# Rope pages and query blocks placed in memory that is free during the prompt attention, first page gathers issued there, and 16-row page gathers for some decode samples

## What is computed

```python
c_past = cache_kv_latent[i][page_table].reshape(db, past, KV_LORA)    # KV_LORA = 256
kr_past = cache_k_rope[i][page_table].reshape(db, past, ROPE_DIM)     # ROPE_DIM = 32
q_abs = jnp.einsum('bthn,chn->bthc', q_nope, w_uk)
s_past = jnp.einsum('bthc,bsc->bhts', q_abs, c_past) + jnp.einsum('bthr,bsr->bhts', q_rope, kr_past)
p = jax.nn.softmax(concatenate([s_past, s_new], -1) * scale, axis=-1)
o_lat = jnp.einsum('bhts,bsc->bthc', p[..., :past], c_past) + ...     # then times w_uv
```

## Time and profile before

| | |
|---|---|
| median of 3 runs | 1027.24 us (1026.8 to 1029.7) |
| profiled execution | 1029.6 us |
| its span | 1027.7 us |
| granted clock, mean of the span | 0.983 |
| busy share of the span: PE, DVE, ACT, POOL | 95%, 65%, 38%, 4% |
| prompt attention of the last head pair ends (DVE, attn_T) | 409.2 us |
| first score product of the sample loop | 415.74 us |
| last weighing of the sample loop | 533.9 us |
| indirect gathers: bytes, share of the 16 DMA engines over the span | 37.75 MB, 9.8% |

### The profile page before, as it was taken

The page is one execution under the profiler, slowest core; times in us unless marked ns, Lnnn a source line. Parts: engine busy times, 40 slices in busy tenths (PEclk is TensorE's granted clock), DMA queues, the critical chain, the costliest instruction groups (busy, mean ns, idle before and its releaser), DMA issues.

```text
span 1027.7 us, 22122 instructions
## 1 busy us (share of the span) xinstructions
PE 974.2 (95%) x9086; PEld 898.9 (87%) x9086; DVE 666.5 (65%) x1054; ACT 387.2 (38%) x857; POOL 39.1 (4%) x44
## 2 busy tenths in 40 slices
PE   4899999999999999599999999999999999999995
PEld 3899999988888897455569999999999999999995
DVE  7467556765555555888837658697774335767567
ACT  4234332324151514333323323556661124565331
POOL 0000000000000011333100000000000000000000
PEclk9899999999999999899999999999999999999998
DMA  9504444313233324999643934224323243341643
GB/s 256 169 24 106 122 122 108 89 23 102 50 96 85 105 102 158 383 344 354 243 161 118 281 85 125 82 82 115 90 82 93 81 114 83 94 111 56 190 119 124
DMA packets 174772, 136.88 MB, mean 133 GB/s; under 512 B 18707, under 2 KB 162936, under 8 KB 170328
## 3 DMA queue, kind: packets, MB, share of 16 engines
q1 hardware_dynamic: 166442, 93.47, 32.5%
q0 software_dynamic: 5760, 37.75, 9.8%
q10 hardware_dynamic: 2502, 4.68, 1.2%
HBM read 124.18 MB, written 11.80 MB: 132 GB/s over the span
## 4 chain that ended last, share of the span: by engine, by line
PE 78%; DVE 12%; issue 4%; ACT 3%; DMA 1%; ACTq 0%; DVEq 0%; another core or an unknown queue 0%; POOL 0%; POOLq 0%
PE PS L2014 34%; PE PS L2242 8%; PE PS L2694 8%; PE PS L2756 6%; PE PS L2025 3%; PE PS L2471 3%; DVE w_lo L1225 2%; PE PS L2589 2%; PE PS L2414 2%; ACT p_sample L972 2%; PE PS L2279 1%; PE PS L2268 1%; PE PS L2340 1%; DVE y_tok L1734 1%; PE PS L2256 1%
## 5 line engine op out<-in xcount | busy, mean ns | idle before, releaser
L2014 PE MATMUL PS<-x_hi,w_hi 128*128 128x262 f32 (+1 forms) x744 | 164.0, 292 | 2.7 <-DVE x_lo L1272 1.4
L1225 DVE TENSOR_TENSOR w_lo<-w_raw,w_hi 128x2048 fp32r<-128x2048 f32 (+3 forms) x65 | 125.9, 1937 | 59.7 <-ACT w_hi L703 48.2
L2014 PE MATMUL PS<-x_lo,w_hi 128*128 128x262 f32 (+1 forms) x744 | 160.0, 287 | 0.0
L2014 PE MATMUL PS<-x_hi,w_lo 128*128 128x262 f32 (+1 forms) x744 | 159.6, 286 | 0.0
L703 ACT ACTIVATE w_hi<-w_raw 128x2048 fp32r<-128x2048 f32 (+3 forms) x59 | 94.5, 1601 | 145.9 <-PE PS L2014 88.3
L2014 PEld LDWEIGHTS PS<-x_hi,w_hi 128*128 128x128 f32 x744 | 120.7, 190 | 6.0 <-issue 2.4
L2014 PEld LDWEIGHTS PS<-x_lo,w_hi 128*128 128x128 f32 x744 | 120.1, 190 | 0.0
L2014 PEld LDWEIGHTS PS<-x_hi,w_lo 128*128 128x128 f32 x744 | 120.0, 190 | 0.0
L2242 PE MATMUL PS<-x_hi,w_hi 128*128 128x262 f32 (+1 forms) x256 | 78.7, 307 | 0.0
L2242 PE MATMUL PS<-x_hi,w_lo 128*128 128x262 f32 (+1 forms) x256 | 73.3, 286 | 0.0
L2242 PE MATMUL PS<-x_lo,w_hi 128*128 128x262 f32 (+1 forms) x256 | 73.3, 286 | 0.0
(11 more groups left out here) (376 smaller groups left out, 2293.2 us busy)
## 6 DMA issues: line engine op xcount, KB each, us to landing
w_raw<-in_w_ffn_in_dram SPq DMA_DIRECT2D x44, 512.0 KB, 4.5
w_raw<-in_w_in_dram SPq DMA_DIRECT2D x37, 512.0 KB, 6.7
w_raw<-in_w_ffn_out_dram SPq DMA_DIRECT2D x28, 320.0 KB, 3.8
w_raw<-in_w_o_dram SPq DMA_DIRECT2D x12, 512.0 KB, 5.2
w_raw<-in_w_ffn_out_dram SPq DMA_DIRECT2D x16, 384.0 KB, 3.9
gate_scratch<-gate_out ACTq DMA_DIRECT2D x8, 524.0 KB, 2.9
gates<-gate_scratch SPq DMA_DIRECT2D x8, 524.0 KB, 9.0
x_T_scratch<-x_sum_T SPq DMA_DIRECT2D x1, 2144.0 KB, 7.5
```

The source lines that it names most:

```text
L1225: V.tensor_tensor(WL[:, at_, ks], RAW[:, at_, ks], WH[:, at_, ks].bitcast(F32), ALU.subtract).then_inc(s_wsplit, 1)
L2014: last = T.matmul(PS[:, bank, 0:n], w[:, par, kw + k, m * P:(m + 1) * P], x[:, k0 + k, half * n:(half + 1) * n], start=start and k == 0 an ...
```

## The change

Rope pages (PGR) and what lies behind them move up by 672 bytes, to 66208, behind q_heads. QBD leaves this row and goes behind the plan of the prompt attention (e3b), where nothing else lies; the gap that pages_c_first needed goes. A third table of row numbers, IDX4, is made for rows of 16 tokens, and `chunk_quad(b, c)` fetches four chunks with one indirect DMA, 16 KB for each partition, 2.1 MB in all. `chunks_in(b)` says which samples use it: 0, 3, 4, 6 and 7. Samples 1, 2 and 5 keep pairs.

On POOL, sample 0 is fetched by two gathers (the second after the 4th normalisation of the last head pair), rope page 0 follows at once, then pairs 0 and 4 of sample 1 after the 8th normalisation, pairs 2 and 6 after the 10th, and rope page 1 after the attention. From sample 2 the order is as before, with the waits for as many chunks as the gather brings; rope page b still stands behind the gather that brings chunks 2 and 3. On ACT the waits for the two gate stores move from the head of `spread_query` behind `stage_query(0)`. On DVE the memset of the new-token columns moves ahead of chunks 1 to 3 and has a count of its own, so that PE may start the scores before the gate stores have landed; PE waits for the other memset (`rows_set` 2) before the first weighing.

```diff
--- before.py
+++ after.py
@@ -115,6 +115,7 @@
             m[32 * g + HEADS + h, 86 + h] = 1.0
             if g < 3:
                 m[32 * g + h, 66 + h] = 1.0
+    m[:, 74:76] = 2 * (i % 4)[:, None] + np.arange(NCH // 4)[None, :]
     m[:, 82:86] = 4 * (i % 4)[:, None] + np.arange(NCH // 2)[None, :]
     c["small"] = m
     return c
@@ -207,6 +208,7 @@
         PTI = fixed("page_table_rows", [P, DEC], I32)
         IDX = fixed("page_rows", [P, DEC, NCH + 1], I32)
         IDX2 = fixed("page_pair_rows", [P, DEC, NCH // 2], I32)
+        IDX4 = fixed("page_quad_rows", [P, DEC, NCH // 4], I32)
         CN8 = fixed("latent_new_T", [P, 2, DEC])
         KR8 = fixed("rope_new_T", [P, DEC])
         arena = top[0]
@@ -257,13 +259,14 @@
         (EX, PTS), e3 = plan(e2, ("probs", [P, 2, 528]), ("probs_T", [P, 2, NT, P]))
 
         (PGC,), _ = plan(0, ("pages_c", [P, 2, NPAGES, KVL]))
-        (_, CTX, QAB, UV), e3b = plan(e3, ("gap5", [P, 392]), ("c_tok0", [T0, KVL]), ("q_abs", [P, 2, DEC, HEADS]), ("w_uv", [P, 2, 512]))
+        (CTX, QAB, UV), e3b = plan(e3, ("c_tok0", [T0, KVL]), ("q_abs", [P, 2, DEC, HEADS]), ("w_uv", [P, 2, 512]))
         assert PGC.shape[2] * KVL * 4 == 32768
-        (PGR, PB, SSM, OL, SPART, OPART, QBD, RTT), e4 = plan(
-            65536, ("pages_r", [P, 2, NPAGES, ROPE]), ("p_sample", [P, 2, 36, HEADS]),
+        (PGR, PB, SSM, OL, SPART, OPART, RTT), e4 = plan(
+            66208, ("pages_r", [P, 2, NPAGES, ROPE]), ("p_sample", [P, 2, 36, HEADS]),
             ("sm", [P, 2, 48]), ("o_lat", [P, 2, HEADS, DEC]),
-            ("score_parts", [P, 2, P]), ("out_parts", [P, 2 * KVL]), ("q_blocks", [P, 2, 9, 32]),
+            ("score_parts", [P, 2, P]), ("out_parts", [P, 2 * KVL]),
             ("rope_T", [P, 4, NCH, 32]))
+        QBD = at("q_blocks", e3b, [P, 2, 9, 32])
         (QRP,), _ = plan(102752, ("q_spread", [P, DEC, 9, HEADS]))
 
         slot_bytes = 8 * SLOT_W * 4
@@ -273,7 +276,7 @@
         assert 8 * KVL * 4 == slot_bytes
         CT = nc.alloc_sbuf_tensor_at("pages_T", [P, 4, 8, NCH, 32], F32, offset=base)
         assert NCH * 1024 * 4 <= 2 * KT * COLS * 4
-        assert e4 + 8 * KVL * 4 <= e3 + 392 * 4
+        assert e4 + 8 * KVL * 4 <= e3
 
         def page(b, c):
 
@@ -361,14 +364,19 @@
         s_pg = [[sem(f"pages_landed{j}_{c}") for c in range(2, NCH)] for j in range(2)]
         s_pf = [[sem(f"first_pages_landed{j}_{c}") for c in range(2)] for j in range(3)]
 
+        def chunks_in(b):
+
+            return 4 if b % 3 < 2 and b != 1 else 2
+
         def page_sem(b, c):
 
-            c -= c % 2
+            c -= c % chunks_in(b)
             return s_pf[b % 3][c] if c < 2 else s_pg[b % 2][c - 2]
 
         def page_count(b, c):
 
-            return b // 3 + 1 if c < 2 else b // 2 + 1
+            c -= c % chunks_in(b)
+            return b // 3 + 1 if c < 2 else len([d for d in range(b % 2, b + 1, 2) if c % chunks_in(d) == 0])
 
         S = sems
 
@@ -646,6 +654,7 @@
             turned = Count(S["ln_turned"])
             
             pair_rows = ins["cache_kv_latent"][0].rearrange("n (q r) c -> (n q) (r c)", q=16)
+            quad_rows = ins["cache_kv_latent"][0].rearrange("n (q r) c -> (n q) (r c)", q=8)
             rope_rows = ins["cache_k_rope"][0].rearrange("n (q r) c -> (n q) (r c)", q=4)
 
             def chunk_pair(b, c):
@@ -653,6 +662,13 @@
                 nc.gpsimd.indirect_dma_start(
                     out=page_pair(b, c).rearrange("p r c -> p (r c)"), out_offset=None,
                     in_=pair_rows, in_offset=bass.IndirectOffsetOnAxis(ap=IDX2[:, b, c // 2:c // 2 + 1], axis=0)
+                ).then_inc(page_sem(b, c), 16)
+
+            def chunk_quad(b, c):
+
+                nc.gpsimd.indirect_dma_start(
+                    out=PGC[:, b % 3, 4 * c:4 * c + 16, :].rearrange("p r c -> p (r c)"), out_offset=None,
+                    in_=quad_rows, in_offset=bass.IndirectOffsetOnAxis(ap=IDX4[:, b, c // 4:c // 4 + 1], axis=0)
                 ).then_inc(page_sem(b, c), 16)
 
             def rope_page(b):
@@ -663,26 +679,36 @@
 
             pool.wait_ge(S["idx_ready"], 1)
             pool.wait_ge(S["uk_T_ready"], 4)
-            for c in range(0, NCH, 2):
+            for c in range(0, NCH, 4):
                 if c:
                     pool.wait_ge(S["probs_ready"], 6 * NT + c)
-                chunk_pair(0, c)
+                chunk_quad(0, c)
+            rope_page(0)
+            pool.wait_ge(S["out_stored"], 16 * 7)
+            pool.wait_ge(S["probs_ready"], 6 * NT + NCH)
+            chunk_pair(1, 0)
+            chunk_pair(1, 4)
+            pool.wait_ge(S["probs_ready"], 8 * NT)
+            chunk_pair(1, 2)
+            chunk_pair(1, 6)
             attn_done = Count(S["attn_done"], start=1)
             pool.wait_ge(attn_done.sem, attn_done.after(4))
-            pool.wait_ge(S["out_stored"], 16 * 7)
-            rope_page(0)
-            for b in range(1, DEC):
-                for c in range(0, NCH, 2):
+            rope_page(1)
+            for b in range(2, DEC):
+                step = chunks_in(b)
+                for c in range(0, NCH, step):
                     if b >= 3:
-                        pool.wait_ge(S["pv_chunk"], (b - 3) * NCH + c + 2)
+                        pool.wait_ge(S["pv_chunk"], (b - 3) * NCH + c + step)
                     pool.sem_inc(S["go_on"])
                     turned = (b - 1) * NCH + c
                     if turned > 0:
                         pool.wait_ge(S["page_turned"], turned)
-                    chunk_pair(b, c)
-                    if c == 2:
-                        if b >= 2:
-                            pool.wait_ge(S["rope_turned"], b - 1)
+                    if step == 4:
+                        chunk_quad(b, c)
+                    else:
+                        chunk_pair(b, c)
+                    if c + step == 4:
+                        pool.wait_ge(S["rope_turned"], b - 1)
                         rope_page(b)
 
         @block.scalar
@@ -940,8 +966,6 @@
 
             def spread_query():
 
-                for j in range(2):
-                    act.wait_ge(stored[j].sem, stored[j].after(1))
                 nc.scalar.activation(QBD[:].rearrange("p a k c -> p (a k c)").rearrange("p (a c) -> p a c", a=9),
                                      IDENT[:, 0:64].unsqueeze(1).to_broadcast([P, 9, 64]), ACT.Copy, scale=0.0
                                      ).then_inc(chain.sem, 1)
@@ -1005,6 +1029,8 @@
 
             spread_query()
             stage_query(0)
+            for j in range(2):
+                act.wait_ge(stored[j].sem, stored[j].after(1))
             hi(N_MERGE + 1, 4)
             for b in range(DEC):
                 sample_act(b)
@@ -1013,7 +1039,7 @@
 
             hi(N_MERGE + 2, 4)
             outputs_back(DEC - 1)
-            act.wait_ge(S["rows_set"], 2)
+            act.wait_ge(S["rows_set"], 3)
             for k in (slice(0, 2), slice(2, 4)):
                 nc.scalar.activation(AH[:, k], AT[:, k, DEAD:], ACT.Copy).then_inc(S["ab_hi"], 1)
             hi(N_MERGE + 3, 4)
@@ -1070,7 +1096,7 @@
 
             conv_acc, h_ready = Count(S["conv_acc"]), Count(S["h_ready"])
             product, w_sum = Count(S["sum_product"]), Count(S["sums_ready"], start=4)
-            act.wait_ge(S["rows_set"], 3)
+            act.wait_ge(S["rows_set"], 4)
 
             def conv_start(m, f):
 
@@ -1411,6 +1437,8 @@
             lo(N_LAT + 1)
             outputs_back(RH - 1)
             sample_back()
+            V.scalar_tensor_tensor(IDX4[:], PTI[:].unsqueeze(2).to_broadcast([P, DEC, NCH // 4]), 8.0,
+                                   SMALL[:, 74:76].unsqueeze(1).to_broadcast([P, DEC, NCH // 4]), ALU.mult, ALU.add)
             V.scalar_tensor_tensor(IDX2[:], PTI[:].unsqueeze(2).to_broadcast([P, DEC, NCH // 2]), 16.0,
                                    SMALL[:, 82:86].unsqueeze(1).to_broadcast([P, DEC, NCH // 2]), ALU.mult, ALU.add)
             V.tensor_scalar(IDX[:, :, NCH], PTI[:], 4.0, SMALL[:, 24:25], ALU.mult, ALU.add).then_inc(S["idx_ready"], 1)
@@ -1628,11 +1656,11 @@
 
             attn_done = Count(S["attn_done"], start=1)
             dve.wait_ge(attn_done.sem, attn_done.after(4))
+            V.memset(PS[:, 6, 256:264], NEG).then_inc(S["rows_set"], 1)
             for c in range(EARLY, 4):
                 turn_chunk(0, c)
             for j in range(2):
                 dve.wait_ge(S[f"gate_stored{j}"], 16 * (1 + 4))
-            V.memset(PS[:, 6, 256:264], NEG)
             V.memset(PB[:, :, 33:36, :], 0.0).then_inc(S["rows_set"], 1)
             turn_rope(0)
             for c in range(4, NCH):
@@ -2464,6 +2492,8 @@
 
                 par = b % 2
                 if c == 0:
+                    if b == 0:
+                        pe.wait_ge(S["rows_set"], 2)
                     if b >= 2:
                         pe.wait_ge(S["olat_ready"], b - 1)
                 for r in range(0, 4, 2):
@@ -2565,7 +2595,7 @@
```

(2 more changed lines are left out.)

## The result

| | before | after |
|---|---|---|
| median (5 runs each, side by side) | 1028.11 us | 1036.42 us |
| ratio, 95% interval | | 1.0072 [1.0051, 1.0094] |
| profiled execution, its span | 1029.6, 1027.7 us | 1036.53, 1034.5 us |
| granted clock, mean of the span | 0.983 | 0.975 |
| gate store issued to DVE's memset behind it | 407.62 to 413.1 us | 405.33 to 416.70 us |

The change makes the kernel slower by some 8 us. The prediction said 1025.7 us, range 1021.0 to 1030.5, with a chance of 0.14 for slower; the median lies 5.9 us above the range.

What follows compares the result with a forecast made beforehand. The prediction took PE, 78% of the chain, to bound the kernel. Terms -1.1 + 0.2 - 0.6 = -1.5 us gave 1028.1 against the profiled 1029.6 us; shifted to the median, 1025.7 us, range 1021.0 to 1030.5.

Steps and rivals of the forecast that it cites:

- the term for the gate store: Loop start: early rope page gains 2.28 us, store delayed +1.2 by gathers; rope turn 1.1 us earlier, term -1.1 us.
- Rival D: Loop start: the store lands 2.3 us or more later and eats the rope gain; 1026.8, at most 1029.5 us; chance 0.19.
- Rope page early: Sample 0: rope page 0 issued about 388 us, so DVE's 2.28 us wait for it goes.
- The moved waits of ACT (0): Loop start: PE's first half starts earlier but saves nothing by itself; ACT's work behind the waits hides; term 0.
- The large gather's landing (0, bounds 0 and +6): Samples with four-chunk gathers: 2.1 MB lands in 8.0 us, nothing lost up to 8.9 us; term 0.
- rival C: Sample loop: large gathers land late, 10.5 us after issue, adding 6.4 us, 1032.1 us; decided from 8.9 us; chance 0.13.
- The score half of samples with one gather less: Samples 3, 4 and 6: score half takes 1.86 us instead of 2.06, 0.2 us each; term -0.6 us.
- The memset and PE's new wait: Loop start: 0.07 us on DVE hidden behind the store wait, PE's wait met long before the first weighing; term 0.
- The 0.2 us for the early gathers: Prompt attention: seven gathers issued there, not four, may briefly hold PE or ACT; +0.2 us, bounds 0 and 1.
- rival B: Sample 0: DVE's 2.29 us stand before reading scores goes as well; 1022.7, or 1021.5 us with store unhindered; chance 0.33.

Runs made afterwards that it cites:

- f3_after: The changed kernel itself, run in the fourth group of runs against the kernel before: ratio 1.0076 [1.0051, 1.0101].
- f1_hold: The changed kernel with pairs 2 and 6 of sample 1 and rope page 1 held until both gate stores landed: 1.0030 of the kernel before.
- e4_rope0: The kernel before with the changed memory plan and only rope page 0 issued early, in the prompt attention: 0.9986 [0.9961, 1.0011] of the kernel before.
- e5_spread: The kernel before with the rope page of samples 2 to 7 issued behind the first pair, so no three gathers in a row: 1.0038 [1.0012, 1.0064].
- f4_spread: Later run of the kernel before with rope pages from sample 2 on behind the first pair: 1.0011 [0.9986, 1.0037] of the kernel before.
- e7_quads: The kernel before with large four-chunk gathers for samples 3, 4, 6 and 7 and nothing else changed: 0.9988 [0.9958, 1.0019] of the kernel before.
- f2_pairs: The changed kernel with two chunks per gather from sample 1 on and nothing held back: 1.0043 [1.0022, 1.0063] of the kernel before.
- group 4: Runs of the changed kernel, its held and its pairs version, and the spread kernel, beside the kernel before at 1019.0 us.
- groups 1, 3 and 5: Sets of runs, each with kernels beside the kernel before on one chip; the first is the result's own, the others had it at 1029.1 and 1027.6 us.
- group 6: Runs of the spread kernel, alone and with rope page 0 early, beside the kernel before at 1027.5 us: ratios 0.9983 and 0.9995.
- groups 2 and 4: Two sets of runs, each with four altered kernels beside the kernel before on one chip, which took 1018.1 and 1019.0 us.
- h1_spread: The kernel before with rope pages from sample 2 on behind the first pair, run in the sixth group: 0.9983 [0.9962, 1.0004] of the kernel before.

## Why the prediction was wrong

**The step that failed is the term for the gate store.** It took "+1.2" for the store's delay, out of bounds of 0 and +5.0, by the row of a store beside 1 MB of weights. Measured, the store lands 5.9 us later (11.24 against 5.3), beyond the upper bound even, and the rope turn starts 3.5 us later in place of 1.1 earlier. Three things were missed. The nearest row had 2 KB packets beside weights; gathers bring 8 KB packets, one for each of the store's. The prediction quoted just this from the Trainium skill ("DMA: Bandwidth & Descriptors", Queues, rings and completion order), that queues take turns at packet boundaries, and then let the sum go by bytes. The packet counts (17 beside 18, and 38 beside 28 with the shorter ones) agree with it. Second, the 2.1 MB were not all: rope page 1 and held-back weights also ran ahead of the store or beside it. Third, the bound "waits for all of the 2.1 MB" left out that the store's own start slips too, from 2.0 to 3.7 us.

**What hid behind it failed with it.** Rival D had this mechanism, "the store eats the rope gain", but its upper bound (1029.5) came out of the same 5.0 us. It also priced the loss by the delay alone. The start of the loop lost 4.7 us. 3.5 of these are the rope turn; most of the other 1.2 lie where DVE stands for the scores of sample 0 (3.27 us against 2.29). That the late store makes them too is not shown. The hold experiment gives the price of the late store as 4.4 us at the first sum-spread and 4.7 by the medians (f3_after less f1_hold), the latter with the uncertainty said above.

**Rope page early: right in mechanism, worth nothing measurable.** With nothing beside the store (e4_rope0) the turn starts right behind it, 5.7 us after its issue against 7.9 in e5_spread of the same group, and the ratio is 0.9986 with 1 inside.

**The moved waits of ACT (0) may have cost something.** They let PE run its first half early and then stand idle. In every kernel that has them, held or not, the products of the second half then take 3.2 to 3.6 us, at half clock; without them 2.1 in the kernel before, 1.95 in f4_spread. From the rope turn to the first sum-spread it is 16.3 us in f1_hold and f3_after and 15.6 in f4_spread, 19.6 in the changed kernel and 18.4 before. But e4_rope0 (16.6) and e7_quads (19.9), without the moved waits, are as long, so these 0.7 to 1.2 us are not put down to them. The prediction's reason, that ACT's work hides, does hold: ACT stands another 0.47 us before it reads the first parts.

**The large gather's landing (0, bounds 0 and +6) was sized too low.** The estimate of 8.0 us became 9.0 to 9.4; the Trainium skill's fit ("DMA: Bandwidth & Descriptors", Anatomy of one DMA), 6.8 us for 2.1 MB by the estimate, is further off. By the prediction's own threshold of 8.9 us rival C holds. Its price of 6.4 us was for 10.5. Measured, it is 4.0 us with samples of 11.93 (f3_after less f2_pairs, uncertain by 2 to 3) and nothing that can be seen with samples of 13.2 (e7_quads, 0.9988). C was half right.

**The rest.** The score half of samples with one gather less is 1.86 us as forecast, and full-clock samples are 0.2 us shorter. The memset and PE's new wait cost nothing that shows; no row after has them as a releaser. The 0.2 us for the early gathers cannot be read from the traces. The 2.29 us of rival B did not go: DVE now stands 3.27 us there, and ACT's read begins 0.89 us after the third gather's issue has ended (427.46 plus 0.94, and 429.29), as the prediction's argument against B had it. But in group 4 the same kernel stands only 0.81 us at this place (f3_after), so the rest of it belongs to the stall of the last section and not to the order on POOL alone.

## What to carry to other kernels

In these traces a store on the critical path shared the DMA engines packet by packet with whatever else was queued, so cost a transfer that you move beside it by its packet size, by how long both run, and by how much later the store can start. In this kernel two gathers issued 2.7 and 1.3 us ahead of the store and one behind it about doubled its landing time; holding them back until it was through undid most of that. A prefetch moved into "idle" time must be checked against every transfer that someone waits for then, not against the engines alone. When a gather is made larger, work out its landing from the measured one at the same load with all its bytes, and ask what slack is left on an execution without the stall that hides it.

## What the runs showed of the hardware that was not expected

**Two sample lengths for the same code.** With pairs of chunks in the gathers, samples at full clock take 13.2 us in groups 1, 3 and 5 (13.4 in group 6, with the rope page behind the first pair) and 11.93 in groups 2 and 4, and the kernel before 1027.5 to 1029.1 us against 1018.1 to 1019.0. One chip number showed both, in group 4 and, a quarter of an hour later, in group 5. The difference is a stall of PE of some 1.3 us in each sample that no semaphore explains, in the samples read near the issue of page gathers. In the short kind the DMA engines are busier if anything: h1_spread, 441.69 to 455.09, and then e4_rope0, 450.21 to 462.15 (columns as in the earlier trace rows):

```profile
441.69:455.09 13.40, 12.47 (x261) 7.87 (x261) 11.48 (x16) 4.34 (x26) 4.68 (x6) 1.00 0.95 342
```

```profile
450.21:462.15 11.94, 11.59 (x262) 7.32 (x262) 11.39 (x16) 4.36 (x26) 4.69 (x6) 1.00 0.99 393
```

That speaks against the DMA engines' load as the cause, though a shorter sample also packs the same bytes into less time. What the cause is stays open; that three gathers stand in a row is not (h1_spread), and how instructions reach PE was not tried. The same change cost 0.6 to 0.8% on either kind, but, as far as the groups tell, by different parts: on one the store, on the other the store and the large gathers.

**A dip of the clock costs some 1.5 us.** A sample with a stretch at 0.50 takes 14.4 to 15.0 us in place of 12.9 to 13.2, or 13.3 to 13.5 in place of 11.93, and one sample of e7_quads took 15.8. It comes in other samples in each execution.
